# Spreading the front of tiles 1 and 4 over the gather steps: 1.1 instead of 1.7 in the first 34 steps, 2.62 instead of 2.45 behind them

## The reference, cut to what matters

```python
h = rms_norm(x, g_mix)
qa, ka, va, qb, kb, vb, logf, ga, gb = project_in(h, w_in, b_fgate)
qa, ka = rope(qa, pos), rope(ka, pos)
ya = swa(qa, ka, va, sinks)              # window 128, 8 heads, 2 key heads
yb = fox(qb, kb, vb, cumsum(logf))       # causal, 8 heads, with forget gates
x = x + (sigmoid(ga) * (ya @ w_a_out) + sigmoid(gb) * (yb @ w_b_out)) @ w_out
q = rms_norm(x, g_ffn) @ w_pq            # 8 heads of expert queries
s = q @ sub_keys                         # two halves of 128 keys
s_top, i_top = top_k(s, 16); best, sel = top_k(all 256 sums, 16)
expert = i_top[0] * 128 + i_top[1]       # 16 experts per head, gate = softmax(best)
a = gelu(x_n . u[expert]) * gate         # u, v: 16384 rows of 1024
x = x + sum over 128 experts of a * v[expert]
y = rms_norm(x, g_final)
```

## Time and profile before

| what | value |
|---|---|
| median of 3 runs | 1857.31 us (1855.47 to 1860.15) |
| profiled execution, its own time | 1864.08 us |
| its span from first to last instruction | 1862.0 us |
| PE busy | 1507.7 us (81%) |
| DVE busy | 1149.1 us (62%) |
| ACT busy | 591.9 us (32%) |
| POOL busy | 857.8 us (46%) |
| DMA moved | 725.41 MB, mean 390 GB/s |
| granted TensorE clock, mean | 0.931 |

### The profile page before, as it was taken

The page is one execution under the profiler, slowest core; times in us unless marked ns, Lnnn a source line. Parts: engine busy times, 40 slices in busy tenths (PEclk is TensorE's granted clock), DMA queues, the critical chain, the costliest instruction groups (busy, mean ns, idle before and its releaser), DMA issues. The chain is left out here.

```text
span 1862.0 us, 19885 instructions
## 1 busy us (share of the span) xinstructions
PE 1507.7 (81%) x6297; PEld 833.9 (45%) x6297; DVE 1149.1 (62%) x3124; ACT 591.9 (32%) x1625; POOL 857.8 (46%) x937
## 2 busy tenths in 40 slices
PE   7988888988667878997987689777777777777786
PEld 4446655666435656554655455222322222222222
DVE  2218976655577576665765854534776666677644
ACT  2421233421111233333210211223544444444433
POOL 0003455655466566665655456444333333333331
PEclk9999799999889899988998799989899999999999
DMA  9548999999999999999999999999999999999996
GB/s 348 214 183 327 383 364 412 411 411 401 412 405 411 411 407 412 409 399 411 391 411 411 383 411 394 399 385 382 409 422 422 421 422 420 422 421 421 422 421 263
DMA packets 150582, 725.41 MB, mean 390 GB/s; under 512 B 17840, under 2 KB 19120, under 8 KB 105424
## 3 DMA queue, kind: packets, MB, share of 16 engines
q0 software_dynamic: 129024, 604.04, 80.6%
q1 hardware_dynamic: 19056, 117.55, 16.0%
q10 hardware_dynamic: 2400, 2.58, 0.4%
HBM read 719.16 MB, written 5.00 MB: 389 GB/s over the span
## 5 line engine op out<-in xcount | busy, mean ns | idle before, releaser
L859 POOL DMA_INDIRECT ring<-in_peer_v,idx_v x320 | 302.5, 945 | 295.9 <-PE summed L1243 172.4
L1946 DVE SCALAR_TENSOR_TENSOR ring<-ring,h_psum 128x1024 f32<-128x1024 f32 x256 | 307.5, 1217 | 209.5 <-DMA ring<-in_peer_uv,idx_u 199.4
L1935 DVE SCALAR_TENSOR_TENSOR ring<-ring,h_psum 128x1024 f32<-128x1024 f32 x320 | 381.7, 1213 | 76.4 <-DMA ring<-in_peer_u,idx_u 73.7
L874 POOL DMA_INDIRECT ring<-in_peer_uv,idx_u x256 | 243.2, 950 | 401.3 <-PE bank L1261 199.2
L849 POOL DMA_INDIRECT ring<-in_peer_u,idx_u x320 | 304.1, 950 | 128.0 <-issue 71.9
L1243 PE MATMUL summed<-ring,spread 128*32 128x512 f32 x1280 | 222.3, 719 | 134.8 <-DMA ring<-in_peer_v,idx_v 134.6
L1261 PE MATMUL summed<-ring,hT 128*128 128x512 f32 x512 | 248.3, 621 | 71.9 <-ACT hT L1518 71.5
L1261 PE MATMUL bank<-ring,hT 128*128 128x512 f32 x512 | 248.7, 627 | 70.9 <-ACT hT L1518 70.6
L1261 PEld LDWEIGHTS bank<-ring,hT 128*128 128x128 f32 x512 | 94.2, 195 | 224.5 <-ACT hT L1518 134.1
L1261 PEld LDWEIGHTS summed<-ring,hT 128*128 128x128 f32 x512 | 91.6, 193 | 228.6 <-ACT hT L1518 152.5
L1515 ACT ACTIVATE dots_sb<-dots_sb 128x1 f32<-128x1 f32 x256 | 51.9, 203 | 404.0 <-DVE ring L1946 404.0
(11 more groups left out here) (253 smaller groups left out, 1682.1 us busy)
## 6 DMA issues: line engine op xcount, KB each, us to landing
w_ring<-in_w_pq SPq DMA_DIRECT2D x24, 1152.0 KB, 9.0
w_ring<-in_w_proj SPq DMA_DIRECT2D x24, 1024.0 KB, 8.5
w_ring<-in_w_gate SPq DMA_DIRECT2D x24, 1024.0 KB, 8.5
w_ring<-in_w_z SPq DMA_DIRECT2D x12, 1024.0 KB, 7.0
w_ring<-in_w_out SPq DMA_DIRECT2D x12, 1024.0 KB, 8.4
ring<-in_peer_u,idx_u POOLq DMA_INDIRECT x320, 12.1
ring<-in_peer_v,idx_v POOLq DMA_INDIRECT x320, 11.9
ring<-in_peer_uv,idx_u POOLq DMA_INDIRECT x256, 14.8
```

The costliest lines, as they stand in the source:

```text
L859: nc.gpsimd.indirect_dma_start(v_ring[:, i % RING, :], None, peer_v, bass.IndirectOffsetOnAxis(idx_v[:, n % 2, j:j + 1], 0)).then_inc(v_la ...
L874: nc.gpsimd.indirect_dma_start(uv_ring[:, slot, :], None, peer_uv, bass.IndirectOffsetOnAxis(idx_u[:, g % 2, j:j + 1], 0)).then_inc(row_la ...
L1935: nc.vector.scalar_tensor_tensor(u, u, 1.0, h_psum[:], ALU.mult, ALU.mult, accum_out=dots_sb[:, g % 2, j:j + 1]).then_inc(u_free, 1)
L1946: nc.vector.scalar_tensor_tensor(u, u, 1.0, h_psum[:], ALU.mult, ALU.mult, accum_out=dots_sb[:, g % 2, j:j + 1]).then_inc(row_dotted, 1)
```

## The change

```diff
-RATE_FIRST, RATE_B, RATE_C = 1.7, 2.45, 2.13
+RATE_FIRST, RATE_B, RATE_C = 1.1, 2.62, 2.13
```

## The result

The change makes the kernel slower: 1863.53 us median (1858.57 to 1867.87, 10 runs) against 1854.47 us (1848.37 to 1860.15, 10 runs) of the kernel before beside it. The ratio is 1.0046, 95% interval [1.0032, 1.0061]. The forecast was 1855 us and a range of 1846 to 1867 us, with 0.23 for slower.

The account below looks back on a forecast made before the run. The kernel was taken as bound by the transfer stream of gathers and weights, engines mattering only where it runs dry. Terms of -3.5, -1 and +2 us gave -2.5 us, a median of about 1855 us, range 1846 to 1867 us.

Parts of the forecast that it names:

- Term 1: Steps 0 to 33, bound by DVE: less attention work and fewer waits start step 34 earlier, a gain of 3.5 us.
- What the prediction drew from it for the rest: More of PE's time at 1.2 GHz in the first 34 steps, late first sums, less throttled time behind step 34.
- Term 2: Steps 34 to about 40: the stall at the first sums keeps roughly its length, fewer ACT waits, a gain of 1 us.
- Term 3: Steps 34 to 123: postponed PE work mostly fits into PE's waits for `v` rows, a loss of 2 us.
- these waits are PE's true slack against the transfers: PE's `v` row waits, 10.7 us in 240.3 to 430 us and 23.4 in 430 to 543, can absorb postponed work.
- Rings of 8 cover a lag of some steps: Steps 34 to 123: where PE is late and frees `v` buffers late, the gather rings bridge some steps.
- PE becomes the bound: Slower rival, steps 40 to 88: added work leaves PE no wait for `v` rows; +8.5 us, about 1866 us, chance 0.23.
- The stream fills: Faster rival: gathers run ahead, terms 1 and 2 reach 7.1 and 4.1 us; about 1849 us, chance 0.28.
- The signs named for a wrong forecast: Distance between the two traces growing behind step 124, or slices seven to twelve falling below 400 GB/s.

Follow-up runs that it names:

- late_tail_2: Kernel before up to step 96, then part B as late as in the changed kernel (selection of head 1 ends at step 123): 1860.95 us, ratio 1.0034.
- before_again: The kernel before, unchanged, run again for a second trace at the 1890 us level: 1890.33 us, ratio to before 0.9993.
- after_again: The changed kernel, unchanged, run again for a second trace at the 1890 us level: 1918.28 us, ratio to before 1.0154.

## Why the prediction was wrong

**Term 1 (forecast -3.5 us).** The mechanism held. Step 34 came at 230.6 us, 0.4 us ahead of the stretch named, DVE was busy 61.66 of 65 us and no forget product held it. The size was off: the 7.3 us by which steps 0 to 33 became shorter were worth 0.5 us of lost transfer, because the traffic stayed at 370 GB/s where 380 to 400 was expected. I had counted one weight piece as postponed, 1.05 MB; 2.8 MB were, 1.2 MB of weights and 1.6 MB of gathers, fewer of which had landed when step 34 began. A stretch that is shortened at the same rate of transfer wins nothing. The clock there went from 0.81 to 0.76 with less for PE to do: the sentence of the Trainium skill ("TensorE: Matmul & The Clock Gate", Part 1: The HAM clock gate), by which activity releases the clock, agrees with the trace there. What the prediction drew from it for the rest didn't come: the clock in steps 34 to 63 was 0.93 against 0.95, not higher, and the first sums came early. One reading was off: from 191.57 to 211.22 us are 19.6 us without a load, not "20 us and more". PE's longest wait after was 14.1 us for `weights_sb`, and the projection behind it ran slow:

```profile
227.97 0.34 PE L1221 MATMUL bank<-const,weights_sb 128*32 128x32 f32 x8 [14.10 <-DVE weights_sb L1955]
228.24 6.22 PE L942 MATMUL bank<-w_ring,hT 128*64 128x256 f32 x16
...
237.51 1.92 PE L1243 MATMUL summed<-ring,spread 128*32 128x512 f32 x16
```

**Term 2 (forecast -1 us).** Better than forecast. The sums came at 237.51 us, not about 242, and the ninth `v` gather on POOL came at 239.73 us, not 243 to 247, after a wait of 3.35 us where 5 to 8 were expected and 6.18 were before:

```profile
239.73 0.94 POOL L859 DMA_INDIRECT ring<-in_peer_v,idx_v  x1 [3.35 <-PE summed L1243]
```

Steps 34 to 63 lose 0.0 us instead of 4.0. It was the upper end of the term, "all 4.1 us gained".

**Term 3 (forecast +2 us) failed in size, and the sum had no term for what came behind it.** In steps 64 to 126, where term 3 stands, the loss rose by 6.3 us (5.6 in steps 64 to 95, 0.7 in 96 to 126): inside its ends of 0 and 10 us, but three times what was taken. Behind step 127 it rose by 8.3 us (5.4 in steps 127 to 135, 2.9 in 136 to 319), and the prediction has nothing there: "The change alters nothing before step 2 and nothing from step 124 on", and two traces that run in parallel. This is the larger failure, and late_tail_2 shows it alone: with the plan altered in steps 97 to 123 only, it costs 0.34%.

In term 3 the step that failed is "these waits are PE's true slack against the transfers". The slack that was to pay for the work was hardly drawn on. PE's waits for `v` rows after, in 240.3 to 430 us and in 430 to 560 us, to set beside the earlier trace rows (10.7 and 23.4 us):

```profile
PE summed L1243 <- DMA ring<-in_peer_v,idx_v: 7.5, 2, 4.7
...
PE summed L1243 <- DMA ring<-in_peer_v,idx_v: 20.8, 3, 7.0
PE h_psum L1099 <- DVE ring L1935: 9.1, 1, 9.1
```

Expected were 0 to 6 and about 12 us. Summed over 100 steps there was room; in the three groups up to step 73 there was not, since PE took 41.1 us for them against 30.5 us of transfer. "Rings of 8 cover a lag of some steps" held before (35.6 us, nothing lost), but not for twice the lag. The wait of PE for DVE behind step 127 was in no term: I had PE's waits before the change, where it shows as 1.57 us, and took "nothing from step 124 on" for the places of the items, while DVE arrived at step 127 4.8 us later than before. That step 123 would come within 5 us of 540 us held (543.75), and said nothing about it, since the selection of head 1, now in step 123, stands right behind its dot product.

**The sum**: -0.5 for term 1, -4.0 for term 2, +6.3 for term 3 and +8.3 for what had no term is +10.1 us, against 9.1 us measured. Forecast was -2.5. That term 1 gave 3.0 us less and term 2 3.0 us more than forecast is luck: the two cancel.

**The rivals.** "PE becomes the bound" had the right sign and nearly the price (+8.5 against +9.1 us), but not the reason. It was to decide when PE waits for no `v` row any more, and PE still waits 7.5 us. With half of part B's larger products left out the cost stayed (1.0058), though PE's time in the place of the hole hardly fell. "The stream fills" came true in steps 34 to 63 alone. The signs named for a wrong forecast did appear: the eighth slice at 362 GB/s, and the distance of the traces grew from 4.8 us at step 127 to 7.4 us at step 320.

**On the HBM limit** near 358 GB/s for a core (the Trainium skill, "DMA: Bandwidth & Descriptors", "Where 436 GB/s comes from"): the trace after again holds 412 GB/s over 97.9 us, so the measurement decides against it here too.

## What to carry to other kernels

Slack summed over a hundred steps says nothing about a plan: cut the trace at each release of the buffers (here every four steps), write down the engine's work between two releases beside the transfer time of the same steps, and add up over the groups that follow each other how far the engine falls behind. A single group over its transfer time cost nothing here (12.9 against 10.2 us); three in a row that were 10.6 us over did. When work is postponed, ask which fixed hand-over stands at the end, and whether the engine that must finish first arrives later there. A stretch that gets shorter is a gain only if the bytes per us rise in it, so compare MB, not steps.

## What the hardware showed

- Work that was taken away came back in part through the granted clock: with half of part B's large products left out, it fell from 0.95 to 0.83 in 240 to 430 us, and PE was busy only 19.5 us less (from the kernel before, 0.95 to 0.85 and 26.2 us).
- A small delay can show up far away: over 300 us behind the last change of the plan, in steps 232 to 239, the clock was 0.72 instead of 0.88, and the traffic 345 instead of 381 GB/s.
- The same kernel took 1890 us in three sets of runs and 1855 in two, and the change cost 1.54% there and 0.46 to 0.52% here. In all twelve traces at the 1890 us level DVE stops without a releaser in the trace, 37 to 68 us in all in steps 34 to 126 (stops of 0.5 us and more), 54.3 us in before_again and 60.6 us in after_again; in the eight traces at the 1855 us level there is none in these steps. The longest, in after_again:

```profile
380.89 0.30 DVE L1849 TENSOR_TENSOR bank<-bank,const 128x128 f32<-128x128 f32 x1 [11.34 <-remote]
```

"remote" means that the trace has no releaser on this core's engines. The cause of these stops is open, and so is whether they are why the change costs more there.
